# Reordering the queues around the gate pairs, and the PSUM units of the squares, in a two-layer encoder trunk

## The reference, cut to what matters

```python
gates = jax.nn.sigmoid(gl).reshape(B, S, N_BRANCH, D_MODEL)      # gl = h @ w_in[:, C_GL:]
merged = (gates[:, :, 0] * (y_ml @ p['w_br_mlstm'])
          + gates[:, :, 1] * (y_sg @ p['w_br_gmlp'])
          + gates[:, :, 2] * (y_sw @ p['w_br_swa']))
x = x + g1 * rms_norm(merged @ p['w_out'], p['g_post_mix'])
h2 = rms_norm(x, p['g_pre_ffn']) * (1 + sc2) + sh2
```

## Time and profile before

| | |
|---|---|
| median of 3 runs | 2051.38 us (2051.14 to 2052.01) |
| the profiled execution | 2051.14 us, span of its instructions 2049.3 us |
| PE busy | 2017.6 us, 98% of the span |
| DVE, ACT, POOL busy | 1105.2, 687.5, 1040.4 us |
| mean granted TensorE clock | 0.997 |

### The profile page before, as it was taken

How to read it: one execution, slowest core, us unless ns; L and a number is a source line. 1 busy time by engine, 2 the same in 40 slices (tenths; PEclk the granted TensorE clock), 3 DMA queues, 4 the chain that set the end, 5 groups by cost and what they waited for, 6 DMA issues and landing times.

```text
span 2049.3 us, 38703 instructions
## 1 busy us (share of the span) xinstructions
PE 2017.6 (98%) x16121; PEld 1944.4 (95%) x16121; DVE 1105.2 (54%) x1769; ACT 687.5 (34%) x1476; POOL 1040.4 (51%) x552
## 2 busy tenths in 40 slices
PE   8999999999999999999999999999999999999998
PEld 7998898999999999999999989889999999999997
DVE  5222466467647545647563245664765573647473
ACT  4111224123334342425532111341243343525253
POOL 0444454565673736354734544546648445354543
PEclk9999999999999999999999999999999999999999
DMA  9746222223351443323544342222234312232332
GB/s 362 260 138 63 56 80 58 69 72 94 94 189 37 137 127 88 89 79 102 175 141 146 62 63 82 58 59 75 72 93 136 122 52 83 83 93 84 92 94 77
DMA packets 300093, 211.94 MB, mean 103 GB/s; under 512 B 14048, under 2 KB 294160, under 8 KB 296720
## 3 DMA queue, kind: packets, MB, share of 16 engines
q1 hardware_dynamic: 293168, 205.94, 34.8%
q10 hardware_dynamic: 6752, 3.53, 0.7%
HBM read 204.65 MB, written 4.07 MB: 102 GB/s over the span
## 4 chain that ended last, share of the span: by engine, by line
PE 92%; DVE 2%; DMA 2%; POOL 2%; ACT 1%; issue 1%; SPq 0%; DVEq 0%; POOLq 0%; ACTq 0%
PE ps L1063 36%; PE ps L1155 20%; PE ps L1091 13%; PE ps L1782 5%; PE ps L1175 3%; PE ps L1181 2%; DMA raw<-in_w_in 2%; PE ps L1308 1%; PE ps L1223 1%; PE ps L1523 1%; PE ps L1687 1%; PE ps L1650 1%; PE ps L1538 1%; PE ps L1665 1%; PE ps L1202 1%
## 5 line engine op out<-in xcount | busy, mean ns | idle before, releaser
L1063 PE MATMUL ps<-h_hi,hi_lo 128*128 128x288 f32 x2560 | 464.4, 299 | 0.3 <-POOL hi_lo L962 0.3
L959 POOL TENSOR_TENSOR hi_lo<-raw,consts 128x1024 fp32r<-128x1024 f32 (+1 forms) x112 | 222.2, 1984 | 449.7 <-PE ps L1063 313.6
L1063 PEld LDWEIGHTS ps<-h_hi,hi_lo 128*128 128x128 f32 x2560 | 381.4, 190 | 8.2 <-issue 5.3
L990 POOL TENSOR_TENSOR a_lo<-raw,a_hi 128x512 fp32r<-128x512 f32 x108 | 159.9, 1481 | 270.6 <-ACT a_hi L2363 270.6
L962 POOL TENSOR_TENSOR hi_lo<-raw,hi_lo 128x1024 fp32r<-128x1024 f32 (+1 forms) x112 | 279.3, 2494 | 8.8
L1063 PE MATMUL ps<-h_lo,hi_lo 128*128 128x288 f32 x1280 | 274.7, 296 | 0.0
L1063 PEld LDWEIGHTS ps<-h_lo,hi_lo 128*128 128x128 f32 x1280 | 207.1, 189 | 0.0
L1091 PE MATMUL ps<-yf_hi,fo_h 128*128 128x288 f32 x704 | 152.3, 298 | 2.9 <-DVE yf_lo L2538 2.9
L1091 PE MATMUL ps<-yf_hi,fo_l 128*128 128x288 f32 x704 | 150.7, 296 | 0.0
L1091 PE MATMUL ps<-yf_lo,fo_h 128*128 128x288 f32 x704 | 150.4, 295 | 0.0
L959 POOL TENSOR_TENSOR hx<-raw,consts 128x1024 fp32r<-128x1024 f32 x26 | 52.2, 2006 | 145.8 <-PE ps L1181 63.6
(11 more groups left out here) (450 smaller groups left out, 5102.2 us busy)
## 6 DMA issues: line engine op xcount, KB each, us to landing
ada<-in_w_ada SPq DMA_DIRECT2D x23, 2048.0 KB, 9.2
raw<-in_w_in SPq DMA_DIRECT2D x88, 512.0 KB, 3.8
raw<-in_w_ffn_in SPq DMA_DIRECT2D x144, 256.0 KB, 3.1
raw<-in_w_ffn_out SPq DMA_DIRECT2D x32, 384.0 KB, 3.4
raw<-in_w_in SPq DMA_DIRECT2D x40, 256.0 KB, 3.8
raw<-in_w_ffn_out SPq DMA_DIRECT2D x32, 320.0 KB, 3.1
raw<-in_w_out SPq DMA_DIRECT2D x16, 512.0 KB, 3.8
raw<-in_w_ffn_in SPq DMA_DIRECT2D x16, 512.0 KB, 4.8
```

What stands on the lines that cost most here:

```text
L959: pool.tensor_tensor(hi, RAW[s][:, 0:size], ONES[:, 0:1].to_broadcast([128, size]), ALU.mult).then_inc(chunk_hi, 1)
L990: pool.tensor_tensor(lo[:, :], RAWB[o], hi[:, :].bitcast(f32), ALU.subtract).then_inc(s_alo, 1)
L1063: m = pe.matmul(o[:, h, :], a[:, k, c0:c0 + 128], mv(k, h), start=(k == 0 and begins), stop=(k == nk - 1 and a is wl))
```

## The change

Three edits, each once per layer.

1. `with_squares`: the list was wo0, wo1, wo2, q1, wo3, q2, wo4, q3, wo5, q4, wo6, q5, q6, wo7 and becomes wo0, wo1, q1, wo2, q2, wo3, q3, wo4, q4, wo5, q5, wo6, q6, wo7. In wo7 the first token sum stands before step k=3 instead of k=5.
2. First pair (p = 0): ACT makes the high parts of the three blocks first and then those of the sums. DVE does low 1 ahead of merge(1,4), and sum 4 and low 2 ahead of merge(1,5).
3. Close pair (p = 3): ACT's `gate_sum_high(1)` for pair 4 stands before `gate_keep(2)` of pair 3 instead of behind it. DVE's low 1 of pair 4 stands before `gate_c22` of pair 3.

```diff
@@ with_squares
-        out += [f"{tile}{i}"] + ([f"{p}q{i - 1}"] if 2 <= i < 7 else []) + ([f"{p}q6"] if i == 6 else [])
+        out += [f"{tile}{i}"] + ([f"{p}q{i}"] if 1 <= i < 7 else [])
@@ PE, output projection
-                                  between={5: x[0], 6: x[1], 7: x[2]} if i == 7 else None)
+                                  between={3: x[0], 6: x[1], 7: x[2]} if i == 7 else None)
@@ ACT
-                for o, i in (("a11", 1), ("a12", 2), ("a22", 3)):
+                for o in ("a11", "a12", "a22"):
                     gate_block_high(o, 0)
+                for i in (1, 2, 3, 4):
                     gate_sum_high(i, 0)
-                gate_sum_high(4, 0)
                 for p, bn in enumerate(GPAIRS):
                     close = bn == (2, 4)
                     gate_keep(0, p)
                     if close:
                         gate_block_high("a11", p + 1)
                     gate_keep(1, p)
+                    if close:
+                        gate_sum_high(1, p + 1)
                     gate_keep(2, p)
                     if close:
-                        gate_sum_high(1, p + 1)
                         gate_sum_high(2, p + 1)
@@ DVE, before the first pair (n == 4)
                         gate_weights(3, 0)
+                        gate_weights_low(1, 0)
                     merge(1, n)
...
-                        gate_weights_low(1, 0)
+                        gate_weights(4, 0)
+                        gate_weights_low(2, 0)
                     merge(1, n + 1)
...
-                gate_weights(4, 0)
-                gate_weights_low(2, 0)
                 gate_weights_low(3, 0)
                 gt_low(3, T3L, GT3SUM[:, :, :], T3H)
                 gate_weights_low(4, 0)
@@ DVE, close pair
                         gate_weights(2, p + 1)
+                        gate_weights_low(1, p + 1)
                         gate_c22(p)
-                        gate_weights_low(1, p + 1)
```

## The result

The change made the kernel slower: 2060.92 us (2059.71 to 2061.68, 5 runs) against 2051.38 us of the kernel before (2048.66 to 2052.39, 5 runs). The ratio is 1.0051, 95% interval 1.004 to 1.0062. I had forecast 2057.3 with a range to 2060.4: the direction is right, the size is 3.6 us short, and the measured time lies 0.5 outside the range. Over all 18 recorded runs of the kernel after, the times go from 2059.70 to 2064.37 with a median of 2061.4; the execution profiled here took 2063.65.

A forecast was written before the change was run, and what follows sets the result against it. PE, busy 98% of the span, was taken as the bound. Terms of 2.30, 0.37 and 0.37 gave 3.04 per layer, 6.1 for two, on 2051.14; with 0.24 to the median it said 2057.3, range 2054.4 to 2060.4.

The forecast's parts named there:

- Price 0.90 forecast: Last step of wo2: PE waits for DVE's read of wo1, whose unit wo3 takes over; +0.90 per layer.
- gain 0.53 forecast: In wo7: the first token sum no longer waits for DVE's read of wo6; 0.53 gained per layer.
- net 0.37 forecast: Output projection: edit 1's price less its gain, +0.37 per layer.
- so what matters is how much sooner sum 4 comes: First pair, PE's hole in p5: the keep follows sum 4's high part, with sum 4 done 0.37 sooner.
- -0.37: First pair: sum 4, its high part, gate_keep(0) and PE all move up by 0.37 per layer.
- a hole of 2.30: Close pair before p7: gate_keep(2) waits behind ACT's high part of pair 4's sum 1; +2.30 per layer.
- +0.74: First pair before p3: PE waits 0.67 for low 4, delayed by POOL's split, plus 0.07 restart.
- POOL's split gets ahead of the 128x1152 low part: First pair, rival: p7 waits 2.0 and p3 another 1.1, 2.5 more per layer; chance 0.13 for one or both layers.
- my own order: First pair: DVE's 128x1152 low part starts before POOL's split, which then goes ahead of low 4.
- POOL's low part meets the sum in any case: Close pair: DVE's sum 1 of pair 4 takes 1.42 instead of 0.68 because it overlaps POOL's low part of a11.
- the stall of edit 3 takes in the others: Close pair, rival: DVE's sum does not move with PE, absorbing the first pair's 0.37; 2056.5, no separate chance.
- The bound that I put on gains (2.4 us): All edited parts: if every PE wait there vanished and nothing opened, the gain would be about 2.4 us.

The follow-up runs named there:

- squares_wo3: Kernel before with edit 1, but wo3 left on wo0's unit and the token sum at k=3; 2049.82 us in one run.
- close_only: Kernel before with edit 3 alone; median 2057.66 us, ratio 1.0028.
- close_act_only: Kernel before with only ACT's half of edit 3, the high part of sum 1 ahead of the third keep; 2060.0 us in one run.
- first_warm14: Kernel before with edit 2 and 14 unread matmuls on PE ahead of p5's last matmul in the first pair; 2052.68 us, ratio 1.0006.
- first_merge_ahead: Kernel before with edit 2, but both merges ahead of sum 4 on DVE; 2055.33 us over 8 runs, ratio 1.0023.
- best: Kernel before with wo3-on-wo0 squares list, first pair's first keep before sum 4's high, pair 4's a11 high after pair 3's third keep; 2049.12 us, ratio 0.999.
- first_dve_only: Kernel before with only DVE's new order of edit 2, ACT as before; 2058.59 us in one run.
- first_dve_merge: Kernel before with DVE's early low 1 but both merges ahead of sum 4, ACT as before; 2051.16 us in one run.
- close_dve_only: Kernel before with only DVE's half of edit 3, low 1 of pair 4 ahead of gate_c22; 2051.85 us in one run.

## Why the prediction was right or wrong

**Edit 1: right.** Price 0.90 forecast, a hole of 0.91 seen; gain 0.53 forecast, 0.55 measured alone (squares_wo3); net 0.37 forecast, 0.39 and 0.36 measured.

**Edit 2: the step that failed.** I wrote that `gate_keep(0)` "stands behind the high part of sum 4", and "so what matters is how much sooner sum 4 comes", and gave -0.37. The first half was true of the kernel before; the edit moved merge(1,5) behind low 2, and the keep also waits for that merge, by its own code. I read what had released the keep in the trace of before and did not list everything that it waits for. The sum did come sooner, by 0.14, and the keep 1.67 later. Under it, the -0.37 also took for granted that nothing idles: low 1 was asked for at 472.70, 0.09 later than reckoned (470.08+2.53), it did not get in ahead of POOL's second low part (it took 1.75; I had it start after the first low part and end near 470.8+2.53 = 473.3), and DVE stood idle 1.21 with its old filler, merge(1,4), queued behind.

**The clock: not in the sum at all.** 2.9 of the 9.5 us are matmuls at the lower clock (a granted clock of 0.51 and 0.50 in the rows above) behind the two holes of the first pair. The granted clock is 1.00 in these stretches of the kernel before, where PE's longest wait is 1.2, so no row of it showed this price; but I had forecast a hole of 2.30, longer than any in the rows on these pairs, and should have kept an end for it in the range. close_only and close_act_only show that even edit 3 as forecast would have cost 1.5 more in one of its layers.

**Low 4 against POOL: the meeting right, the wait absent.** I gave +0.74 for low 4 behind POOL's split, and as a rival the case that POOL's split gets ahead of the 128x1152 low part. In layer 0 the rival's order happened: POOL asked at 479.22, DVE at 479.29, and DVE needed 3.05 and 2.87 for what takes 1.35 and 0.69. In layer 1 my own order happened, DVE 0.14 ahead:

```profile
1487.97 1.35 DVE L2539 TENSOR_TENSOR h_lo<-t_sum,h_hi 128x1152 fp32r<-128x1152 f32 x1
1489.24 2.38 DVE L2539 TENSOR_TENSOR g_s_lo<-g_s_sum,g_s_hi 128x512 fp32r<-128x512 f32 x1
```
```profile
1488.11 2.96 POOL L959 TENSOR_TENSOR hi_lo<-raw,consts 128x1024 fp32r<-128x1024 f32 x1 [3.83 <-DMA raw<-in_w_br_swa]
```

The 128x1152 low part took its 1.35, and low 4 took 2.38 where I had reckoned 2.37 (477.78 to 480.15). That agrees with the Trainium skill, "SBUF — State Buffer", section "Who interferes with whom", by which issue order decides who blocks; 0.07 us behind or 0.14 ahead did it here. But in neither layer did PE wait. In layer 0 PE, late and slow, came to the last matmul of p7 at 485.54, 0.41 after low 4 was ready at 485.13. At full clock, 1.4 sooner, it would have waited for about 1.0, and so it does: 1.03 in first_warm14, 1.08 in first_merge_ahead. The rival had 3.1. In layer 1 low 4 was ready at 1491.62. PE resumed at 1488.08, and the 36 matmuls up to that point take 4.8 at 0.133 each, so it would not have waited at full clock either: the hole alone had taken the wait in.

**Edit 3: price right, sum wrong.** Alone and at full clock it costs 2.27 (2.30 forecast), all of it by ACT's order, as argued. Within the change it costs 0.97 and 1.29. The step that failed is the sentence "POOL's low part meets the sum in any case", with the start of the sum that I had moving with PE. From before to after PE is 5.6 later there in layer 0 (2.53 at the start of the first pair, 3.10 in it), while DVE's sum 1 of pair 4 is 5.0 later (530.75 to 535.77) and POOL's low part 4.1 (530.33 to 534.39), since ACT's high of a11 ahead of it waits for a DMA and not for PE. So the sum runs after POOL's operation (0.69 in place of 1.42), which saves 0.7, and starts sooner by PE's time, which saves 0.6: the hole is 1.0. In layer 1 the sum moves with PE but for 0.2, and what is saved is nearly all the meeting with POOL (0.69 in place of 1.50). The rival "the stall of edit 3 takes in the others" had the second part, and let it take in 0.37; the meeting with POOL it had not. I had treated the terms as independent because they lie 55 us apart; but what a late PE finds done depends on queues and transfers that do not move with it.

**How the total came within 3.4 us.** Forecast 6.1, measured 9.46: +5.7 on edit 2 (3.5 holes and 2.9 clock, less the 0.7 forecast) and -2.3 on edit 3. Two errors of opposite sign, so that the miss is no larger is luck and no credit to the sum. The forecast also has a slip in its last step: 2051.14+6.08 is 2057.22, and with the 0.24 up to the median it is 2057.5, not 2057.3. The bound that I put on gains (2.4 us) holds; best gets 2.0.

What stays open: what in layer 0 or 1 decides whether the clock falls behind a hole of 2.4 to 2.5, and why the untouched stretches vary by up to 3 us between executions. The second bears on the single runs (first_dve_only, first_dve_merge, squares_wo3, close_act_only, close_dve_only), of which only the stretches can be used.

## What to carry to other kernels

Before moving an instruction past another, list every wait of the things behind it from the code, not only the releaser that the trace shows: the one that came last before the change says nothing of the second to last. Ask of each idle gap on a helper engine which instruction now fills it, and keep that one in front. Where the bounding engine would stand still as long as the holes of 2.4 us and more that lowered its clock here, price the clock too, and do not add up prices of stalls that share the same helper queues: run the parts alone and together.

## What the runs showed of the hardware

- TensorE's granted clock behind a hole in a dense stream (128x288 matmuls, one every 0.133; the holes are idle times of PEld). Behind holes of 2.28 (first_dve_only), 2.31 (close_only), 2.34 (first_merge_ahead) and one of 2.51 (close_act_only, layer 1) it stayed at 1.00. Behind 2.41 (close_act_only, layer 0), another of 2.51 (close_only, layer 1), 2.62 and all longer ones in the gate pairs it fell to the lower level, with matmuls 0.24 apart, and cost 1.3 to 1.6 each time. It can fall some time after PE has resumed: at once in layer 0 of the kernel after, 1.4 us later in layer 1. With the hole filled (first_warm14) it did not fall in either layer. So between these lengths the hole's length alone does not decide: the same code gave either in its two layers, the longer hole without the fall.
- DVE and POOL in turn on large two-input operations: with both asking all the time, 1.35 became 3.05 and 0.69 became 2.87 on DVE, while POOL's second half took 3.38. In the kernel after, DVE's 128x1152 part started 0.07 behind POOL in layer 0 and took 3.05; in layer 1 it started 0.14 ahead and took 1.35.
- An operation of DVE that begins after POOL's has ended takes its 0.69 again (0.09 us after it, in the close pair). So a delay of the kernel elsewhere can shorten an operation.
